# PEER layer, top-k over 100 candidates instead of 256, and another order of transfers between the U slabs and the V groups

## The reference, cut to what matters

```python
sv, si = lax.top_k(s, PEER_TOPK)                       # per head, two halves
cand_s = (sv[:, :, 0, :, None] + sv[:, :, 1, None, :]) # 16 x 16 candidates
top_s, pos = lax.top_k(cand_s, PEER_TOPK)
experts = take_along_axis(cand_i, pos)                 # 8 heads x 16 experts
gates = softmax(top_s)
hid = gelu(einsum('nkd,nd->nk', u_table[experts], xb)) * gates
y = einsum('nk,nkd->nd', hid, v_table[experts])
```

## Time and profile before

| | |
|---|---|
| median of 3 runs | 3171.16 us (3168.12 to 3172.24) |
| profiled execution | 3174.46 us |
| its span | 3172.7 us |
| mean granted clock of PE | 0.989 of full speed |
| PE busy | 3083.1 us, 97% of the span |
| DVE, ACT, POOL busy | 2085.0, 1165.7, 776.9 us |
| DMA | 542.36 MB, mean 171 GB/s |

### The profile page before, as it was taken

The page is one execution under the profiler, slowest core; times in us unless marked ns, Lnnn a source line. Parts: engine busy times, 40 slices in busy tenths (PEclk is TensorE's granted clock), DMA queues, the critical chain, the costliest instruction groups (busy, mean ns, idle before and its releaser), DMA issues.

```text
span 3172.7 us, 44288 instructions
## 1 busy us (share of the span) xinstructions
PE 3083.1 (97%) x16765; PEld 2723.5 (86%) x16765; DVE 2085.0 (66%) x3509; ACT 1165.7 (37%) x1668; POOL 776.9 (24%) x431
## 2 busy tenths in 40 slices
PE   8999999999999699999999999999999999999998
PEld 7788899999999699999998888888887877788887
DVE  6685459998998577888886574544444354436663
ACT  4443334344544333333333222333323444423322
POOL 2302436533333333444430001000003421231000
PEclk9999999999999899999999999999999999999999
DMA  5201345569999999999942333333323311133322
GB/s 169 79 33 48 93 136 190 155 217 337 323 341 334 325 346 377 377 378 373 385 177 87 99 93 100 93 94 98 97 88 103 93 54 41 40 93 93 97 89 93
DMA packets 188077, 542.36 MB, mean 171 GB/s; under 512 B 17696, under 2 KB 77472, under 8 KB 187296
## 3 DMA queue, kind: packets, MB, share of 16 engines
q1 hardware_dynamic: 150112, 403.59, 38.4%
q0 software_dynamic: 36864, 134.23, 11.5%
q10 hardware_dynamic: 960, 2.65, 0.3%
HBM read 483.76 MB, written 54.53 MB: 170 GB/s over the span
## 4 chain that ended last, share of the span: by engine, by line
PE 76%; DVE 12%; DMA 7%; ACT 3%; issue 1%; SPq 1%; DVEq 0%; ACTq 0%
PE ring_banks L298 20%; PE ring_banks L300 20%; PE ring_banks L299 20%; DMA slot<-u 6%; PE work_banks L298 3%; PE work_banks L299 3%; PE work_banks L300 3%; PE ring_banks L1613 1%; ACT stage L2085 1%; PE work_banks L1582 1%; DVE hot L2806 1%; DMA gates<-stage 1%; PE work_banks L1585 1%; PE ring_banks L1287 1%; DVE hot L2802 1%
## 5 line engine op out<-in xcount | busy, mean ns | idle before, releaser
L298 PE MATMUL ring_banks<-xx,wlo 128*128 128x512 f32 (+2 forms) x2704 | 1003.3, 371 | 28.9 <-DVE wlo L2300 26.5
L300 PE MATMUL ring_banks<-xx,whi 128*128 128x512 f32 (+2 forms) x2704 | 993.6, 367 | 0.0
L299 PE MATMUL ring_banks<-xx,whi 128*128 128x512 f32 (+2 forms) x2256 | 821.8, 364 | 0.0
L1725 ACT ACTIVATE whi<-slot 128x1024 fp32r<-128x1024 f32 x427 | 451.4, 1059 | 932.4 <-DMA slot<-w 572.8
L921 POOL TENSOR_TENSOR wlo<-slot,whi 128x1024 fp32r<-128x1024 f32 x167 | 414.9, 2492 | 1390.7 <-ACT whi L1725 1390.5
L298 PEld LDWEIGHTS ring_banks<-xx,wlo 128*128 128x128 f32 x2704 | 511.6, 189 | 95.3 <-DVE wlo L2300 28.3
L300 PEld LDWEIGHTS ring_banks<-xx,whi 128*128 128x128 f32 x2704 | 510.9, 189 | 63.5
L299 PEld LDWEIGHTS ring_banks<-xx,whi 128*128 128x128 f32 x2256 | 426.8, 189 | 46.9 <-issue 0.2
L2300 DVE TENSOR_TENSOR wlo<-slot,whi 128x1024 fp32r<-128x1024 f32 x260 | 317.4, 1223 | 206.6 <-ACT whi L1725 196.8
L2095 ACT ACTIVATE vhi<-v 128x1024 fp32r<-128x1024 f32 x128 | 135.3, 1061 | 323.9 <-DMA v<-v 322.1
L943 POOL DMA_INDIRECT v_row<-v,row_numbers x128 | 188.0, 1469 | 263.4 <-DVE row_sum L2840 208.3
(11 more groups left out here) (506 smaller groups left out, 4945.1 us busy)
## 6 DMA issues: line engine op xcount, KB each, us to landing
slot<-w SPq DMA_DIRECT2D x301, 512.0 KB, 3.6
slot<-u SPq DMA_DIRECT2D x128, 512.0 KB, 4.8
v<-v SPq DMA_DIRECT2D x128, 512.0 KB, 7.8
early<-early SPq DMA_DIRECT2D x128, 192.0 KB, 4.0
ge<-early SPq DMA_DIRECT2D x32, 768.0 KB, 13.8
gates<-stage SPq DMA_DIRECT2D x47, 512.0 KB, 5.9
gbuf<-gates SPq DMA_DIRECT2D x31, 768.0 KB, 7.8
hT<-xT SPq DMA_DIRECT2D x8, 256.0 KB, 7.2
```

The source lines that it names most:

```text
L298: pe.matmul(out, w[1], x[0], start=start, stop=False)
L299: pe.matmul(out, w[0], x[1], start=False, stop=False)
L300: return pe.matmul(out, w[0], x[0], start=False, stop=stop)
L1725: act.activation(whi[s % RING], slot[s % RING], ACT.Copy).then_inc(whr, 1)
```

## The change

Four things.

The candidate table has 100 columns a head instead of 256: the first three ranks of the first list with all 16 of the second, and the other thirteen with the first four. A position in this shorter table is turned into the two ranks by arithmetic in floating point and a shift, nine instructions in place of three.

The gates of the last 64 tokens for V group 0 are copied from `stage` to `gbuf[0]` directly; their write to memory and read back, and the semaphore `p_g0`, are gone.

The other transfers of the seam are laid between the turns of the tail: `ge[0]`, the copy and three groups of gates behind turn 0, `gbuf[0]` and two pieces behind turn 1, two pieces behind each of the turns 2 and 3, the last piece behind turn 4, and V group 1 behind turns 6 and 7.

V group 0 is prepared ahead: DVE does `apply_gates(0)`, `v_low(0)` and `weight_low(0)` in the last turn of the tail, after the low part of the last slab, and ACT does `weight_high(0)` before the gelu of the last tile. Of the gathered U rows 12 instead of 16 are used in the tail, and 5 instead of 4 in each of the V groups 0 to 3.

```diff
--- before.py
+++ after.py
@@ -48,6 +48,8 @@
 
 PEER_HEADS = 8
 TOPK = 16
+WHOLE, PART = 3, 4
+CANDS = WHOLE * TOPK + (TOPK - WHOLE) * PART
 KEYS = 128
 SLOTS = PEER_HEADS * TOPK
 
@@ -246,7 +248,7 @@
 NORM_AT, _ = _starts(NORMS, 0)
 
 ROW_STEPS = TD // BATCH
-ROWS_IN_TAIL, ROWS_FIRST = 16, 4
+ROWS_IN_TAIL, ROWS_FIRST = 12, 5
 U_RING, V_RING = 4, 6
 GROUPS = KEYS // 4
 
@@ -486,8 +488,9 @@
         sc2 = region("sc2", 2, P)
         sv = region("sv", 16, TOPK)
         si = region("si", 16, TOPK)
-        cand = region("cand", PEER_HEADS, 256)
-        cand2 = region("cand2", 2, 256)
+        cand = region("cand", PEER_HEADS, CANDS)
+        cand2 = region("cand2", 2, CANDS)
+        place_f, rank_f, first_f = [region(f"choice_{x}", SLOTS) for x in ("place", "rank", "first")]
         tops = region("tops", PEER_HEADS, TOPK)
         posu = region("posu", PEER_HEADS, TOPK)
         abu = region("abu", 2, SLOTS)
@@ -683,7 +686,6 @@
         p_om = sem("onehots_multiplied")
         p_st = sem("gates_staged")
         p_gw = [sem(f"gates_written{b}") for b in range(2)]
-        p_g0 = sem("first_gates_of_last_tokens_written")
         p_hw = [sem(f"early_written{b}") for b in range(4)]
         p_v = [sem(f"v_loaded{r}") for r in range(4)]
         p_g = [sem(f"gates_loaded{b}") for b in range(3)]
@@ -852,30 +854,31 @@
                         if r == 0:
                             sp.wait_ge(p_st, STAGE // 4 * t)
                         write_gates(t - 1, r, p_gw[(t - 1) % 2])
-                if t == last:
-                    sp.wait_ge(p_gw[0], (last + 1) // 2 * PIECES * 16)
-                    for r in range(4):
-                        load_v(1, r)
-                    for b in range(4):
-                        sp.wait_ge(p_hw[b], 16)
-                    sp.dma_start(ge[0], a["early"][0:4].rearrange("r p t -> p r t")).then_inc(p_g[0], 16)
                 if t == 0:
                     sp.wait_ge(p_tc, 1 + GT)
                     for r in range(4):
                         load_v(0, r)
+            sp.wait_ge(p_gw[0], (last + 1) // 2 * PIECES * 16)
             sp.wait_ge(p_gw[1], last // 2 * PIECES * 16)
-            sp.dma_start(gbuf[0][:, 0:last], a["gates"][0, :, 0:last].rearrange("i t (r n) -> i t r n", r=4)).then_inc(p_g[0], 16)
-            sp.wait_ge(p_st, STAGE // 4 * (last + 1))
-            sp.dma_start(a["gates"][0, :, last], stage[last % 2][:, 0].rearrange("p r t -> p (r t)")).then_inc(p_g0, 16)
-            sp.dma_start(a["gates"][1:4, :, last].rearrange("g i n -> i g n"),
-                         stage[last % 2][:, 1:4].rearrange("p g r t -> p g (r t)")).then_inc(p_gw[1], 16)
-            write_gates(last, 1, p_gw[1])
-            sp.wait_ge(p_g0, 16)
-            sp.dma_start(gbuf[0][:, last], a["gates"][0, :, last].rearrange("i (r n) -> i r n", r=4)).then_inc(p_g[0], 16)
-            for u in range(KEYS - TAIL, KEYS):
-                next_u(u)
-                if u - KEYS + TAIL + 2 < PIECES:
-                    write_gates(last, u - KEYS + TAIL + 2, p_gw[1])
+            for n in range(TAIL):
+                next_u(KEYS - TAIL + n)
+                if n == 0:
+                    for b in range(4):
+                        sp.wait_ge(p_hw[b], 16)
+                    sp.dma_start(ge[0], a["early"][0:4].rearrange("r p t -> p r t")).then_inc(p_g[0], 16)
+                    sp.wait_ge(p_st, STAGE // 4 * (last + 1))
+                    sp.dma_start(gbuf[0][:, last].rearrange("p r n -> p (r n)"),
+                                 stage[last % 2][:, 0].rearrange("p r t -> p (r t)")).then_inc(p_g[0], 16)
+                    sp.dma_start(a["gates"][1:4, :, last].rearrange("g i n -> i g n"),
+                                 stage[last % 2][:, 1:4].rearrange("p g r t -> p g (r t)")).then_inc(p_gw[1], 16)
+                if n == 1:
+                    sp.dma_start(gbuf[0][:, 0:last], a["gates"][0, :, 0:last].rearrange("i t (r n) -> i t r n", r=4)).then_inc(p_g[0], 16)
+                for c in range(2 * n - 1, min(2 * n + 1, PIECES)):
+                    if c > 0:
+                        write_gates(last, c, p_gw[1])
+                if n >= TAIL - 2:
+                    load_v(1, 2 * (n - TAIL + 2))
+                    load_v(1, 2 * (n - TAIL + 2) + 1)
             sp.wait_ge(p_gw[1], (last // 2 + 1) * PIECES * 16)
             load_gates(1)
             for b in range(4):
@@ -2103,12 +2106,12 @@
 
             act.wait_ge(p_om, TD // 4)
             for u in range(KEYS - TAIL, KEYS):
+                if u == KEYS - 1:
+                    weight_high(0)
                 ahead_gelu(u)
                 if u == KEYS - TAIL:
                     v_high(0)
-            act.wait_ge(p_g0, 16)
             act.wait_ge(p_gw[1], TD // STAGE // 2 * PIECES * 16)
-            weight_high(0)
             for g in range(1, GROUPS):
                 v_high(g)
                 weight_high(g)
@@ -2774,9 +2777,12 @@
                 for x in range(2):
                     step(dve.tensor_copy(sif[:, x], siu4[:, :, x, :].unsqueeze(3).to_broadcast([P, PEER_HEADS, TOPK, 2])))
                 sv4 = sv.rearrange("p (h x) k -> p h x k", x=2)
-                step(dve.tensor_tensor(cand.rearrange("p h (a b) -> p h a b", a=TOPK),
-                                       sv4[:, :, 0, :].unsqueeze(3).to_broadcast([P, PEER_HEADS, TOPK, TOPK]),
-                                       sv4[:, :, 1, :].unsqueeze(2).to_broadcast([P, PEER_HEADS, TOPK, TOPK]), ALU.add))
+                split = WHOLE * TOPK
+                for columns, ranks_a, n in ((slice(0, split), slice(0, WHOLE), TOPK), (slice(split, CANDS), slice(WHOLE, TOPK), PART)):
+                    na = ranks_a.stop - ranks_a.start
+                    step(dve.tensor_tensor(cand[:, :, columns].rearrange("p h (a b) -> p h a b", b=n),
+                                           sv4[:, :, 0, ranks_a].unsqueeze(3).to_broadcast([P, PEER_HEADS, na, n]),
+                                           sv4[:, :, 1, 0:n].unsqueeze(2).to_broadcast([P, PEER_HEADS, na, n]), ALU.add))
                 step.wait()
                 for h in range(0, PEER_HEADS, 2):
                     best16([(cand[:, h + x, :], cand2[:, x, :], tops[:, h + x, :], pos[:, h + x, :]) for x in range(2)])
@@ -2788,11 +2794,22 @@
                                   ALU.subtract).then_inc(p_ge, 1)
 
                 flat = pos.rearrange("p h k -> p (h k)")
-                step(dve.tensor_scalar(ab[:, 0, :], flat, 4, None, ALU.logical_shift_right))
-                step(dve.tensor_scalar(ab[:, 1, :], flat, 15, None, ALU.bitwise_and))
-                step.wait()
-                step(dve.tensor_copy(abf.rearrange("p x h k -> p x (h k)"), ab))
-                step.wait()
+                step(dve.tensor_copy(place_f, flat))
+                step.wait()
+                step(dve.tensor_scalar(rank_f, place_f, -float(split), 0.0, ALU.add, ALU.max))
+                step.wait()
+                step(dve.scalar_tensor_tensor(ab[:, 0, :], rank_f, float(TOPK // PART - 1), place_f, ALU.mult, ALU.add))
+                step.wait()
+                step(dve.tensor_scalar(ab[:, 0, :], ab[:, 0, :], 4, None, ALU.logical_shift_right))
+                step.wait()
+                step(dve.tensor_copy(rank_f, ab[:, 0, :]))
+                step(dve.tensor_copy(abf[:, 0].rearrange("p h k -> p (h k)"), ab[:, 0, :]))
+                step.wait()
+                step(dve.tensor_scalar(first_f, rank_f, float(PART), float(split - WHOLE * PART), ALU.mult, ALU.add))
+                step.wait()
+                step(dve.scalar_tensor_tensor(first_f, rank_f, float(TOPK), first_f, ALU.mult, ALU.min))
+                step.wait()
+                step(dve.tensor_tensor(abf[:, 1].rearrange("p h k -> p (h k)"), place_f, first_f, ALU.subtract))
                 for x in range(2):
                     step.wait()
                     step(dve.tensor_tensor(hot, abf[:, x].unsqueeze(2).to_broadcast([P, PEER_HEADS, TOPK, TOPK]),
@@ -2868,14 +2885,6 @@
                         gate_parts(GT - 1)
 
             onehots()
-            for n in range(TAIL):
-                slab_low(U_AT + KEYS - TAIL + n)
-                for s in U_ROWS_IN_TAIL[n * ROWS_IN_TAIL // TAIL:(n + 1) * ROWS_IN_TAIL // TAIL]:
-                    use_u(s)
-
-            step(dve.memset(wfwf[:, :, 0:1], 1.0))
-            step(dve.tensor_tensor(wfwf[:, :, 1], pcol("fin1", 0, KD), pcol("fin1", 0, KD), ALU.mult))
-
             def apply_gates(g):
                 b = g % 3
                 dve.wait_ge(p_g[b], 32 * (g // 3 + 1) + 16 * (b == 0))
@@ -2897,8 +2906,21 @@
                     dve.wait_ge(p_vh, 4 * g + r + 1)
                     dve.tensor_tensor(vlo[b][:, r, :], vbuf[b][:, r, :], vhi[b][:, r, :].bitcast(F32), ALU.subtract).then_inc(p_vs, 1)
 
+            for n in range(TAIL):
+                slab_low(U_AT + KEYS - TAIL + n)
+                if n == TAIL - 1:
+                    apply_gates(0)
+                    v_low(0)
```

(15 more changed lines are left out.)

## The result

The changed kernel takes 3147.49 us (median of 4 runs, 3146.17 to 3148.22) against 3171.7 for the kernel before, timed on the same chip (median of 4, 3168.12 to 3174.14). The ratio is 0.9924 [0.9907, 0.9941]: 24.2 us faster. The direction was right and the time lies in the wide range (3120 to 3150), 2.5 us from its end, but not in the forecast of 3127 to 3140: of the 37 us only 24 came.

What follows compares the result with a forecast made beforehand. TensorE, busy 97% of the span, bounds the kernel, so only its waits and low clock can be won. Top-k rounds 19 plus seam 18 make 37 us, from 3171.16 to 3134; forecast 3127 to 3140 (0.55), wide range 3120 to 3150.

Steps and rivals of the forecast that it cites:

- B: Rival for the seam: DMA returns the gain as a wait at a V group; seam 9, total 28 us, 3143; chance 0.13.
- C: Rival for the top-k rounds: longer decoding meets POOL more often, a round gains only 3 us; total 29, 3142; chance 0.08.
- Scans, table and decoding: Top-k rounds: shorter scans save 6.4 us, the table 1.1, longer decoding costs 1.4; net 6.1 us a round.
- Stops behind GpSimd: Top-k rounds: added short DVE instructions stand still during POOL's subtractions, costing 0.7 to 2.1 us a round, 1.1 taken.
- ACT's exp comes in time by the same shift: Top-k rounds: ACT's exp of a round, behind eight tiles' gelu, comes in time by the same shift; no cost counted.
- What the rounds are worth on PE: Top-k rounds: 5.0 us shorter rounds just suffice for all three gate waits (2.6, 4.1, 4.7 needed); 19 us taken.
- The order alone: Seam: the new order of transfers alone starts spread(0) near 1094.5 instead of 1117.9, 23 us.
- The bound by DMA time: Seam: 55 us of full DMA remain, V group 1 ready at 1112 earliest, spread(1) at 1119 against 1137.2: 18 us.
- The price of spreading: Seam: pieces between slab loads cost time; if slabs 125 to 127 each took 17.1 us, PE had them no earlier.
- A: Rival for the seam: order alone counts, DMA has room; seam 23 to 30, total 42 to 49 us, 3125; chance 0.15.
- D: Rival at the seam: V group 1 and gates land late, spread(1) after 1156; at 1165 the kernel takes 3180; chance 0.04.
- E: Rival for both places: PE's waits move on to another reason and nothing changes, 3171; chance 0.03.

Runs made afterwards that it cites:

- e1: Kernel before with only the shorter candidate table and its decoding, seam as before: 3160.41 us, ratio 0.9964.
- e3: Changed kernel with the old three-instruction decoding on the table of 100, so other experts are chosen: 3137.08 us, ratio 0.9895.
- e4: Changed kernel with GpSimd writing zeros instead of subtracting for the low parts of the first 48 U slabs: 3134.84 us, a single execution.
- e9: Changed kernel with each GpSimd subtraction on the first 48 U slabs cut into four pieces of 256 columns: 3138.51 us, ratio 0.9888.
- e6: Changed kernel with ACT's exp of round 0 behind six gelus instead of eight: 3142.44 us, ratio 0.9903.
- e10: e9 with the earlier exp of e6 added: 3137.9 us, ratio 0.9893.
- e7: Changed kernel with 16 gathered U rows in the tail and four in each V group 0 to 3, as before: 3149.09 us, ratio 0.993.
- e8: Changed kernel with V group 1 loaded two turns of the tail earlier: 3147.75 us, ratio 0.9925.
- e11: e10 with four gathered U rows instead of five in each of the first V groups: 3136.4 us, ratio 0.9885.
- e13: e11 with the gathered rows of the tail's last turn used ahead of the last slab's low part: 3134.4 us, ratio 0.9881.
- e12: Changed kernel with gathered U rows from number 96 on bringing 128 KB instead of 512 KB: 3134.7 us, ratio 0.9879.

## Why the prediction fell short

The wide range holds the time only because it took in the rivals B and C; the forecast itself gave too much to both parts, 8 us at the top-k rounds and some 3 at the seam.

**Scans, table and decoding (net 6.1 us a round): right.** 24.6 us less work in four rounds, by the count above.

**Stops behind GpSimd ("0.7 to 2.1 us, and I take 1.1"): this is the step that failed.** It measured 3.4 us a round (2.8 in e1), above the upper bound too. In the lines of the decoding alone the stops grew by 2.5 a round (2.0 in e1). The bound rested on "POOL has one instruction per tile". That gives how often POOL reads, 2.4 of every 4.1 us, and not how many stops a chain of short instructions meets. While the chain stands still POOL finishes, and within 1.7 us or so of work the next subtraction begins and stops it again: in the rows of round 2 two stops fall into nine instructions, at L2799 and L2812. Two more places were not in the sum: the table, which as one instruction took 2.28 us and as two takes 1.25 and 1.13 instead of 0.56 and 0.59 (1.25 a round), and L2825, which never was hit before and was hit in a quarter of its executions (1.1 a round). Other lines lost 1.4 a round less. e3, e4 and e9 change this item in three ways, and each time the gates waits go, but for 0.6 us in e3. It follows too that the gain of a shorter chain depends on how it falls between POOL's instructions.

**"ACT's exp comes in time by the same shift": wrong by 2.3 us**, and by 5.7 in e3 and e9, where DVE arrives earlier. What it costs PE is not shown: e6 took the wait away and can't be told from the change, and e10 can't be told from e9.

**What the rounds are worth on PE: the rule right, its input wrong.** 2.2 us instead of 5.0 a round is less than the 2.6, 4.1 and 4.7 that the forecast needed for the three waits, so all three stayed, smaller. e9 supplies a fast enough round and the waits vanish at the forecast time. Rival C (a round gains only 3 us) was the right mechanism; it left the seam as it was and its 29 us are nearer to 24 than my 37. The one-hot stage, said to only move, gave 3.1: PE's waits for oneI (L2875) are 1.1 us in all, 4.1 before.

**Seam: the order as forecast, size off by 2 to 4 us.** The order alone would have given spread(0) at 1094.5 less the 11.6 of the part ahead of it, 1082.9; it came at 1084.57. (The terms that the forecast names, 1066.2 + 16.6 + 6 + 1 + 3, give 1092.8; it doesn't say what the other 1.7 are.) The bound by DMA time said 55 us from the free queue to apply_gates(1); slab 124 went out at 1044.38 and apply_gates(1) began at 1100.76, 56.4. That agrees with DMA time but does not single it out, since the rows and the late issue of `ge` end at the same place. The copy on the chip, for which no row stood, took 10.7 us to land, between the bounds of 2.7 and 17.1, not nearer to the first as forecast, and hidden all the same. DMA issues of after, 1040 to 1125:

```profile
slot<-u SPq DMA_DIRECT2D x5, 512.0 KB, 9.3
...
gbuf<-stage SPq DMA_DIRECT2D x1, 128.0 KB, 10.7
```

The price of spreading is in these rows as well: the last slabs took 9.3 us to land by the median (slab 124 6.8, then 11.8, 9.3 and 10.9), where the forecast had slab 124 land in 5.6. It fell on another slab than forecast: PE waited 5.52 us for slab 125, issued at 1049.38 behind ge and two small pieces, 0.33 for 126 and 2.76 for 127, where the forecast had 0, 6 and 1. Not in the forecast was the clock behind the wait at V group 1, 0.70 from 1108 to 1115, which costs 7 x 0.30 = 2.1 us; the kernel before lost 2.6 in the same way behind its last wait (0.50 from 1117.9 to 1123). Behind the slab waits too it was at its lower level for a while, 0.67 from 1063.5 to 1070 and 0.72 from 1077.4 to 1083.5; tile 127 so took 6.0 us, and only 1.08 us of the 3 us wait for `glo` were left. Rival B (DMA returns the gain at the V groups) holds for the 4.2 us between spread(0) and spread(1), a part of its nine. Rivals A, D and E are out: the share is 1.01, spread(1) is 29 us earlier, and the time moved.

**Open** is how the wait at V group 1 divides into bytes, row latency and the late issue of `ge`. They bind within some 3 us of each other, and no kernel here took more than one away.

## What to carry to other kernels

When DVE gets more, shorter instructions while GpSimd runs long ones that read the SBUF, count each place of the chain where such an instruction can begin, not the share of time: in e3's comparison 5.8 us of added work had brought 7.5 us of stops. Cutting GpSimd's instructions into pieces, though it makes them longer in all, gave 9 us here for four lines. In a stretch where the DMA share is 1.0, moving loads or rows about gave nothing that the runs resolve (e7, e8, e11, e13); fewer bytes gave 7 us (e12).

## What I had not expected of the hardware

- How regular the stops are: in e9 all eight executions of the last selection (what L2825 is in after) took 0.71 us, 0.42 over the minimum, where after had six at 0.29 and two above 2.
- Pieces cost GpSimd little: 4 x 0.74 = 3.0 us by the median for what took 2.4.
- Slabs of 512 KB take 9.3 us to land where the DMA share is 1.01 and 4.9 by the median of the whole kernel, so the landing time of the page is no price for a full stretch.
